# A hybrid encoder layer: nine groups' weight sums begun in the first six slots, and splits of weights moved behind the heads' chains

## The chip, the cores and the metric

The kernel runs on one core of a Trainium2 chip. The metric is the device time of one execution in microseconds (us). The engines are TensorE (PE, matmuls), VectorE (DVE), ScalarE (ACT), GpSimd (POOL) and SyncE (SP, which issues DMAs). They run their own instruction streams in order and wait for each other on semaphores.

## The reference

One layer on 512 prompt tokens and 32 new tokens, 1024 features, with the same weights:

```
h = rms_norm(x) @ w_in             # u, q, k, v (512 each), two gates (1024 each)
A = pooled means of u (windows 2, 4, 8, 16) minus u, a 128x128 map per group, @ w_pool_up
B = stick-breaking attention of 8 heads x 64: z = q k / 8, causal (s < t),
    a[t,s] = exp(log_sigmoid(z) + sum of log_sigmoid(-z) over the keys between s and t), a @ v, @ w_sb_up
x += (sigmoid(gate_a) * A + sigmoid(gate_b) * B) @ w_out
x += relu(rms_norm(x) @ w_up)^2 @ w_down          # 4096 hidden features
x += sigmoid(rms_norm(x) @ w_ple_gate) * (p @ w_ple_proj)
y = rms_norm(x)
```

The new tokens attend to 256 cached keys and to themselves. Keys, values and the pooling state are outputs too.

## The kernel before

Features lie on the partitions and the 544 tokens on the free axis. Every weight tile is 128 x 1024 numbers of fp32 (512 KB). Each is split into a high part in fp32r (an ACT copy, `w_hi`) and a low part (a DVE subtraction, `w_lo`). A product is then three matmul passes: high x high, high x low, low x high. In the code this pair of instructions is `split` (L845 on ACT, L1812 on DVE), with the tile's load in `raw` before it; there are two buffers of `raw` and four of `w_hi` and `w_lo`, so splits run three tiles ahead (`AHEAD`).

The first stage runs over four pairs of heads (`pair(i)`), each with eight weight tiles. Between its tiles TensorE computes, for each head hh of the pair:
- `scores` (L1381, L1382): z;
- `sums` (L1394 to L1406): the sums of the stick-breaking logs, as products with a triangle of -1;
- `outputs` (L1420, L1422): the product with the values.

The other engines run a chain between them. After the scores ACT computes a logarithm in three passes (`chain`, L921 to L925) and DVE makes the stick (`stick`, L1898). POOL masks its four diagonal blocks (`mask_diagonals`, L767). ACT and DVE make the high and low parts (`stick_hi` L930, `stick_lo` L1913 and L1915), and TensorE takes them up in `sums`. Then ACT takes the exponent (`prob`, L938), POOL masks it (L767 again), and ACT and DVE split it (`prob_hi` L943, `prob_lo` L1919) for `outputs`. Between these, ACT and DVE hold the splits of weights, in an order that is written out by hand in `pair`.

After the pairs come the pooling projection, the attention of the new tokens (POOL's mask L807, TensorE's sums L1559 to L1564), the projections and the mlp. Up and down projections (three of the four chunks) and the last gate use a 2x2 scheme with seven products in place of eight. For it, sums of quarters of the weights are needed. There are 16 groups (`SUM_GROUPS`), and in each four sums S1 to S4, which POOL has made by DMAs in device memory (`sums_t`): step 0 is four copies, steps 1 to 3 are two, one and one additions (DMAs that accumulate). Step k + 1 of a group needs step k landed. POOL issues them in slots. Slot k is issued in the loop over heads after the second mask of head k (k below 8), and later at paces set by TensorE. `sum_copies(k)` waits for all DMAs of the slots before k (`sums_made(k - 1)`), then the copies and the additions of slot k are issued. In the loop, the pooling means (`window_sums`, `window_mean`) stand around them:

```
for g in range(HEADS):
    pool.wait_ge(sp_done, g + 1)
    mask_diagonals(spm_done)
    ...
    pool.wait_ge(prob_done, g + 1)
    mask_diagonals(pm_done)
    sum_copies(g)
    sum_additions(g)
```

SP loads a finished sum like any weight tile, once the slot of its last step has landed (L679).

Of the kernel before, what the change touches and what calls it, by code (L numbers as in the profile page):

```python
# [19 lines left out]
HEADS = 8  # L20
# [12 lines left out]
S1_PER = 8  # L33
# [13 lines left out]
AHEAD = W_RING - 1  # L47
# [41 lines left out]

SUM_GROUPS = tuple((what, 2 * c + e) for c in range(CHUNKS) for what in ("up", "dn") if what == "up" or c < SEVENS  # L90
                   for e in range(2)) + (("ple", 0), ("ple", 1))

SUM_PAD = 16

# [203 lines left out]
def hybrid_step_kernel(nc, w_tiles, x_t, p_t, ck_t, cv, state_t, w_grp, vecs,  # L298
# [5 lines left out]
    with ctx:  # L304
# [217 lines left out]
        sums_in = sem("sums_in")  # L522
# [98 lines left out]

        def sum_slot(k):

            return [(i, k - i) for i in range(max(0, k - len(SUM_STEPS) + 1), min(k + 1, len(SUM_GROUPS)))]

        def sums_made(k):

            return 16 * sum(len(SUM_STEPS[step]) for j in range(k + 1) for _, step in sum_slot(j))
# [8 lines left out]
        def _(sp):  # L637
# [35 lines left out]
            def staged(n):  # L673
                name = STAGED_LOADS[n]
                wait_free(n)
                group, what = group_side(name) or (None, None)
                if what in SUMS:
                    nth = SUM_GROUPS.index(group)
                    sp.wait_ge(sums_in, sums_made(nth + len(SUM_STEPS) - 1))  # L679
                    sp.dma_start(raw_buf(n), sums_t[len(SUMS) * nth + SUMS.index(what), :, :])\  # L680
                        .then_inc(raw_in[raw_at(n)], 16)
                elif name[0] == "p":
                    sp.dma_start(raw_buf(n)[:, 0:TOK], p_t[:, name[1], :]).then_inc(raw_in[raw_at(n)], 16)
                else:
                    sp.dma_start(raw_buf(n), w_tiles[stored_tile(name), :, :]).then_inc(raw_in[raw_at(n)], 16)
# [21 lines left out]
        def _(pool):  # L707
# [104 lines left out]
            for c in range(CHUNKS):  # L812
                second = [NTH[("dn", c, s, 0)] for s in (0, 4)] if c < SEVENS else [NTH[("down", c, q)] for q in (0, 4)]
                paces += [(NTH[("up", 2 * c, 0)], NTH[("up", 2 * c + 1, 0)]), tuple(second)]
            for k, (copies, additions) in enumerate(paces, HEADS):
                if copies:
                    pool.wait_ge(full, copies)
                sum_copies(k)
                if copies:
                    pool.wait_ge(full, additions)  # L820
                sum_additions(k)
# [11 lines left out]
        def _(act):  # L833
# [126 lines left out]
            def pair(i):  # L960
# [18 lines left out]
                    split(AHEAD + 1)  # L979
                if not first:  # L980
                    prob(1, i - 1)
                split(AHEAD + 2, i, S1_PER, 2)
                if not first:
                    prob_hi(1, i - 1)
                chain(0, i)
                split(AHEAD + 3, i, S1_PER, 3)
                stick_hi(0, i)
                act.wait_ge(taken, 3 + i * S1_PER)
                act.dma_start(v_t[i, :, :], ev[:, 2, 0:TOK]).then_inc(kv_out[1], 16)
                act.wait_ge(vt_done, i + 1)  # L990
# [9 lines left out]
                    mean_hi(1)  # L1000
                split(AHEAD + 5, i, S1_PER, 5)
                prob(0, i)
                split(AHEAD + 6, i, S1_PER, 6)
                prob_hi(0, i)
                if last:
                    group_hi(0)
                    group_hi(1)
# [2 lines left out]
                    mean_hi(2)  # L1010
                    mean_hi(3)
                chain(1, i)
                split(AHEAD + 7, i, S1_PER, 7)
                if last:
                    group_hi(2)
                    group_hi(3)
                stick_hi(1, i)

            pair(0)
            with act.Fori(1, PAIRS - 1) as i:  # L1020
# [778 lines left out]
        def _(dve):  # L1799
# [189 lines left out]
            def pair(i):  # L1989
# [22 lines left out]
                else:  # L2012
# [5 lines left out]
                    dve.wait_ge(taken, 2 + i * S1_PER)  # L2018
                    dve.tensor_copy(kst[:, i, :], k[:, SEQ:TOK])
                    k_parts(i)  # L2020
                    split(AHEAD + 2, i, S1_PER)
                    prob_lo(1, i - 1)
                    dve.wait_ge(kv_out[1], 16 * i)
                    normed(2, v, i, S1_PER, pair_result(2, i)).then_inc(taken, 1)
                    dve.wait_ge(taken, 3 + i * S1_PER)
# [1 line left out]
                if not first:  # L2027
                    head_out(1, i - 1)
                    stick(0, i)
                    split(AHEAD + 3, i, S1_PER)  # L2030
                    stick_later(0, i)

                if not first:
                    pool_input(i)
                if first:
                    stick(0, i)
                    split(AHEAD + 3)
                    stick_later(0, i)
                stick_lo(0, i)
                dve.wait_ge(vhi_done, i + 1)  # L2040
                dve.tensor_tensor(v_parts[:, :, V_LO, :], o_heads, v_parts[:, :, V_HI, :], ALU.subtract)\
                   .then_inc(vlo_done, 1)
# [4 lines left out]

                    dve.wait_ge(mean_done, GROUPS)
                gate(1, i)
                split(AHEAD + 6, i, S1_PER)  # L2050
                if last:
                    mean_lo(0)
                    mean_lo(1)
                prob_lo(0, i)
                gate(2, i)
                if last:
                    group_lo(0)
                head_out(0, i)
                if last:
                    group_lo(1)  # L2060
                    mean_lo(2)
                    mean_lo(3)
                    gate(3, i)
                else:
                    split(AHEAD + 7, i, S1_PER)
                stick(1, i)
                if last:
                    group_lo(2)
                    group_lo(3)
                    stick_later(1, i)  # L2070
                    split(AHEAD + 7, i, S1_PER)
                    stick_lo(1, i)
                    for s in kv_out:
                        dve.wait_ge(s, 16 * PAIRS)
                else:
                    gate(3, i)
                    stick_later(1, i)
                    stick_lo(1, i)

            pair(0)  # L2080
            with dve.Fori(1, PAIRS - 1) as i:
# [472 lines left out]
```

## Time and profile before

| | us |
|---|---|
| median of 3 runs | 772.89 (772.16 to 772.94) |
| the profiled execution | 772.34 |
| its span | 770.6 |
| PE busy | 754.8 |
| DVE busy | 556.9 |
| ACT busy | 422.0 |
| POOL busy | 147.2 |

The span is the time from the first instruction to the last, and the profiled execution's own time lies 1.7 us above it. TensorE's granted clock over the span is 0.996 of full. POOL is seldom busy, but it issues 128 DMAs of 512 KB each for the sums; they have 35.5% of the 16 DMA engines' time over the span, and the queue of SP, mostly weight loads, has 35.6%.

### The profile page before, as it was taken

What the parts mean: (1) busy time and instruction counts of PE and PEld (TensorE: products, weight loads), DVE (VectorE), ACT (ScalarE), POOL (GpSimd) and SP (SyncE); (2) the same over time, 40 slices, a digit from 0 to 9 for tenths busy, and PEclk for the clock granted to TensorE, in tenths of its full rate; (3) what the DMA queues carried; (4) which work ended last, traced back from release to release, by engine and by line L of the source; (5) the groups of instructions that cost most, each with busy time, mean ns of one, the idle gap of its engine ahead of it and who ended that gap; (6) DMA issues with size and microseconds to landing.
All of it is one profiled execution on the core that took longest, in us unless ns stands there. A gap on an engine that the chain in (4) does not pass through costs nothing.

```text
span 770.6 us, 14459 instructions
## 1 busy us (share of the span) xinstructions
PE 754.8 (98%) x5902; PEld 746.2 (97%) x5902; DVE 556.9 (72%) x705; ACT 422.0 (55%) x524; POOL 147.2 (19%) x259
## 2 busy tenths in 40 slices
PE   9999999999999999999999999999999999999994
PEld 9999999999999999999999999999999999999993
DVE  6776556566567527588998669965998667677986
ACT  7545535435485442477674347634763356556575
POOL 1051342453471332021110111111101000000001
PEclk9999999999999999999999999999999999999998
DMA  7254848769779899988797989789776957342503
GB/s 242 93 181 140 233 147 224 225 193 262 218 179 265 259 242 275 292 267 262 213 299 270 236 329 251 282 232 354 207 243 201 278 185 217 105 117 66 204 1 116
DMA packets 49516, 165.78 MB, mean 215 GB/s; under 512 B 6320, under 2 KB 8368, under 8 KB 49456
## 3 DMA queue, kind: packets, MB, share of 16 engines
q1 hardware_dynamic: 28512, 94.16, 35.6%
q0 software_dynamic: 18688, 67.18, 35.5%
q10 hardware_dynamic: 2256, 3.60, 1.4%
q8 instruction: 43, 0.70, 0.4%
q14 instruction: 17, 0.14, 0.1%
HBM read 160.39 MB, written 71.63 MB: 301 GB/s over the span
## 4 chain that ended last, share of the span: by engine, by line
PE 90%; DVE 5%; ACT 3%; issue 1%; DMA 1%; SPq 0%; POOL 0%; POOLq 0%; DVEq 0%
PE psum L1646 23%; PE psum L1697 16%; PE psum L1345 14%; PE psum L1351 14%; PE psum L1348 14%; PE psum L1394 1%; PE psum L1422 1%; DMA xt<-x_t 1%; PE psum L1420 1%; PE psum L1382 1%; PE psum L1381 1%; ACT xt L1265 1%; PE psum L1401 1%; PE psum L1406 1%; ACT L879 0%
## 5 line engine op out<-in xcount | busy, mean ns | idle before, releaser
L853 ACT ACTIVATE w_hi<-raw_more 128x1024 fp32r<-128x1024 f32 x83 | 87.7, 1056 | 72.3 <-PE psum L1697 43.3
L1345 PE MATMUL psum<-a_hi,w_hi 128*128 128x272 f32 x576 | 120.6, 291 | 0.6 <-DVE w_lo L1812 0.5
L1820 DVE TENSOR_TENSOR w_lo<-raw_more,w_hi 128x1024 fp32r<-128x1024 f32 x83 | 101.1, 1222 | 26.1 <-ACT w_hi L853 25.7
L1351 PE MATMUL psum<-a_hi,w_lo 128*128 128x272 f32 x576 | 119.3, 289 | 0.0
L1348 PE MATMUL psum<-a_lo,w_hi 128*128 128x272 f32 x576 | 118.9, 288 | 0.0
L1646 PE MATMUL psum<-u_hi,w_hi 128*128 128x272 f32 x560 | 116.4, 289 | 1.0 <-ACT h_of L1097 1.0
L1646 PE MATMUL psum<-u_hi,w_lo 128*128 128x272 f32 x560 | 115.8, 289 | 0.0
L1646 PE MATMUL psum<-u_lo,w_hi 128*128 128x272 f32 x560 | 115.7, 288 | 0.0
L1345 PEld LDWEIGHTS psum<-a_hi,w_hi 128*128 128x128 f32 x576 | 90.3, 189 | 1.1 <-DVE w_lo L1812 0.7
L1348 PEld LDWEIGHTS psum<-a_lo,w_hi 128*128 128x128 f32 x576 | 90.5, 189 | 0.0
L1351 PEld LDWEIGHTS psum<-a_hi,w_lo 128*128 128x128 f32 x576 | 90.0, 189 | 0.0
L1646 PEld LDWEIGHTS psum<-u_hi,w_hi 128*128 128x128 f32 x560 | 87.9, 188 | 1.7 <-issue 1.2
L1646 PEld LDWEIGHTS psum<-u_lo,w_hi 128*128 128x128 f32 x560 | 88.3, 189 | 0.0
L1646 PEld LDWEIGHTS psum<-u_hi,w_lo 128*128 128x128 f32 x560 | 87.4, 188 | 0.0
L1812 DVE TENSOR_TENSOR w_lo<-raw,w_hi 128x1024 fp32r<-128x1024 f32 x41 | 51.2, 1250 | 43.3 <-ACT w_hi L845 43.1
L1820 DVE TENSOR_TENSOR w_lo<-raw,w_hi 128x1024 fp32r<-128x1024 f32 x44 | 53.6, 1222 | 19.2 <-ACT w_hi L853 12.3
L789 POOL DMA_DIRECT2D sums_t<-sums_t x32 | 27.5, 1013 | 207.1 <-PE psum L1646 87.9
L1348 PE MATMUL psum<-b_lo,w_hi 128*128 128x272 f32 x304 | 62.9, 288 | 0.0
L853 ACT ACTIVATE w_hi<-raw 128x1024 fp32r<-128x1024 f32 x39 | 41.2, 1056 | 36.0 <-PE psum L1697 21.6
L1345 PE MATMUL psum<-b_hi,w_hi 128*128 128x272 f32 x288 | 60.0, 290 | 0.0
L782 POOL DMA_DIRECT2D sums_t<-w_tiles x64 | 33.6, 535 | 135.5 <-DMA sums_t<-w_tiles 97.7
L1351 PE MATMUL psum<-b_hi,w_lo 128*128 128x272 f32 x288 | 59.4, 287 | 0.0
(287 smaller groups left out, 1553.0 us busy)
## 6 DMA issues: line engine op xcount, KB each, us to landing
sums_t<-w_tiles POOLq DMA_DIRECT2D x96, 512.0 KB, 8.2
raw<-w_tiles SPq DMA_DIRECT2D x63, 512.0 KB, 4.4
raw_more<-sums_t SPq DMA_DIRECT2D x42, 512.0 KB, 5.8
raw_more<-w_tiles SPq DMA_DIRECT2D x41, 512.0 KB, 4.5
sums_t<-sums_t POOLq DMA_DIRECT2D x32, 512.0 KB, 11.1
raw<-sums_t SPq DMA_DIRECT2D x22, 512.0 KB, 6.0
xt<-x_t SPq DMA_DIRECT2D x8, 272.0 KB, 5.7
y_t<-xt SPq DMA_DIRECT2D x16, 136.0 KB, 1.9
```

The lines of the kernel that those rows point to most:

```text
L782: pool.dma_start(sum_tile(i, what), sum_tile(i, of)).then_inc(sums_in, 16)
L789: pool.dma_start(sum_tile(i, what), sum_tile(i, of), accum_op=ALU.add).then_inc(sums_in, 16)
L853: act.activation(w_hi[:, t % W_RING, :, :].rearrange("p k c -> p (k c)"), src, ACT.Copy)\
L1265: act.activation(x, x, ACT.Copy, scale=g_fin[:, m:m + 1]).then_inc(xg_last, 1)
L1345: pe.matmul(base[:, h, :], w_hi[:, s, wk, :], at(hi, k, h * HALF, (h + 1) * HALF), start=(opens and q == 0), stop=False, skip_group_check= ...
L1348: pe.matmul(base[:, h, :], w_hi[:, s, wk, :], at(lo, k, h * HALF, (h + 1) * HALF), start=False, stop=False, skip_group_check=True)
L1351: mm = pe.matmul(base[:, h, :], w_lo[:, s, wk, :], at(hi, k, h * HALF, (h + 1) * HALF), start=False, stop=(closes and q == len(ks) - 1), s ...
L1381: pe.matmul(z, b_lo[:, keys], b_hi[:, both], start=(b != 3), stop=False, skip_group_check=True)
L1646: mm = pe.matmul(out[:, two, :], w_part[:, t % W_RING, 2 * k + two, :], u_part[:, op, k, :], start=(OPENS[s] and k == 0 and w_part is w_hi ...
L1697: mm = pe.matmul(out[:, two, :], w_part[:, t % W_RING, 2 * k + two, :], h_part[:, i * HALF:(i + 1) * HALF], start=(OPENS[s] and k == 0 and ...
L1812: dve.tensor_tensor(w_lo[:, s, :, :].rearrange("p k c -> p (k c)"), raw[:, t % RAW_RING, :], w_hi[:, s, :, :].rearrange("p k c -> p (k c)" ...
L1820: dve.tensor_tensor(w_lo[:, t % W_RING, :, :].rearrange("p k c -> p (k c)"), src, w_hi[:, t % W_RING, :, :].rearrange("p k c -> p (k c)"), ...
```

## The change

Group i began its four steps in slot i. A table now says in which slot each group begins: groups 0 to 8 begin in slots 0, 1, 2, 2, 3, 3, 4, 5, 5, and from group 11 on it is as before. The number of slots stays at 19. SP's wait for a sum follows the table.

```diff
+BEGINS = (0, 1, 2, 2, 3, 3, 4, 5, 5, 7, 9, 11, 12, 13, 14, 15)
+SLOTS = BEGINS[-1] + len(SUM_STEPS)
...
-            return [(i, k - i) for i in range(max(0, k - len(SUM_STEPS) + 1), min(k + 1, len(SUM_GROUPS)))]
+            return [(i, k - at) for i, at in enumerate(BEGINS) if 0 <= k - at < len(SUM_STEPS)]
...
-                    sp.wait_ge(sums_in, sums_made(nth + len(SUM_STEPS) - 1))
+                    sp.wait_ge(sums_in, sums_made(BEGINS[nth] + len(SUM_STEPS) - 1))
...
-            for k, (copies, additions) in enumerate(paces, HEADS):
+            for k, (copies, additions) in zip(range(HEADS, SLOTS), paces):
```

On ACT, in `pair`:

```diff
                 if not first:
                     prob(1, i - 1)
-                split(AHEAD + 2, i, S1_PER, 2)
+
                 if not first:
                     prob_hi(1, i - 1)
+                split(AHEAD + 2, i, S1_PER, 2)
                 chain(0, i)
+                stick_hi(0, i)
                 split(AHEAD + 3, i, S1_PER, 3)
-                stick_hi(0, i)
...
                 prob(0, i)
+                prob_hi(0, i)
                 split(AHEAD + 6, i, S1_PER, 6)
-                prob_hi(0, i)
...
                 chain(1, i)
-                split(AHEAD + 7, i, S1_PER, 7)
...
                 stick_hi(1, i)
+                split(AHEAD + 7, i, S1_PER, 7)
```

On DVE the same four splits go behind `prob_lo(1, i - 1)`, `stick_lo(0, i)`, `prob_lo(0, i)` and `stick_lo(1, i)`.

Two places in the order of instructions. First POOL, in the loop over heads, from the second mask of head 4 to the first mask of head 6 (`work`). The `sums_t` rows are slots 4 and 5, and the `gates` and `upad` rows are a pooling mean. Before:

```order
L767 AFFINE_SELECT work<-work 128x128 x4
L782 DMA sums_t<-w_tiles 128x1024 x4
L789 DMA sums_t<-sums_t 128x1024 x2
L789 DMA sums_t<-w_tiles 128x1024 x2
L757 TENSOR_SCALAR gates<-gates 128x551
L758 TENSOR_TENSOR gates<-gates,invc 128x8
L760 TENSOR_TENSOR upad<-gates,upad 128x559
L767 AFFINE_SELECT work<-work 128x128 x8
L782 DMA sums_t<-w_tiles 128x1024 x4
L789 DMA sums_t<-sums_t 128x1024 x2
L789 DMA sums_t<-w_tiles 128x1024 x2
L767 AFFINE_SELECT work<-work 128x128 x4
```

The same stretch of POOL now (the lines have moved down by four):

```order
L771 AFFINE_SELECT work<-work 128x128 x4
L786 DMA sums_t<-w_tiles 128x1024 x4
L793 DMA sums_t<-sums_t 128x1024 x3
L793 DMA sums_t<-w_tiles 128x1024 x4
L761 TENSOR_SCALAR gates<-gates 128x551
L762 TENSOR_TENSOR gates<-gates,invc 128x8
L764 TENSOR_TENSOR upad<-gates,upad 128x559
L771 AFFINE_SELECT work<-work 128x128 x8
L786 DMA sums_t<-w_tiles 128x1024 x8
L793 DMA sums_t<-sums_t 128x1024 x4
L793 DMA sums_t<-w_tiles 128x1024 x2
L771 AFFINE_SELECT work<-work 128x128 x4
```

Slot 4 has 11 DMAs where it had 8, and slot 5 has 14 where it had 8; the masks stand where they stood.

Second ACT, in the last pair, from the exponent of head 5 (L938) to the parts of head 6's stick. `w_hi` is a split of weights, the wide `b_hi` a high part, `work` the chain. Before:

```order
L938 ACTIVATE work<-psum 128x1280
L845 ACTIVATE w_hi<-raw 128x1024
L943 ACTIVATE b_hi<-work 128x1280
L921 ACTIVATE work<-psum 128x1280
L923 ACTIVATE work<-work 128x1280
L925 ACTIVATE work<-work 128x1280
L845 ACTIVATE w_hi<-raw 128x1024
L930 ACTIVATE b_hi<-work 128x1280
L932 ACTIVATE later_hi<-later 128x384
L989 DMA v_t<-ev 128x544
```

The same stretch of ACT now:

```order
L942 ACTIVATE work<-psum 128x1280
L947 ACTIVATE b_hi<-work 128x1280
L849 ACTIVATE w_hi<-raw 128x1024
L925 ACTIVATE work<-psum 128x1280
L927 ACTIVATE work<-work 128x1280
L929 ACTIVATE work<-work 128x1280
L934 ACTIVATE b_hi<-work 128x1280
L936 ACTIVATE later_hi<-later 128x384
L849 ACTIVATE w_hi<-raw 128x1024
L994 DMA v_t<-ev 128x544
```

Both splits have moved from ahead of an instruction that waits for POOL's mask to behind it.

## Rows read from the trace of the kernel before

**Rows 1.** The page's busy time of each engine.
```profile
PE 754.8 (98%) x5902; PEld 746.2 (97%) x5902; DVE 556.9 (72%) x705; ACT 422.0 (55%) x524; POOL 147.2 (19%) x259
```

**Rows 2.** Waits of PE: line <- releaser: us in total, times, longest.
```profile
PE psum L1345 <- issue: 1.1, 1, 1.1
...
PE psum L1345 <- DVE w_lo L1812: 0.5, 1, 0.5
```

**Rows 3.** DMA queues (packets, MB, share): 53:82, 82:111.5, then 140.4:169.9 us.
```profile
q0 software_dynamic: 576, 2.10, 20.9%
...
q0 software_dynamic: 928, 3.16, 40.2%
...
q0 software_dynamic: 1216, 4.21, 58.0%
q1 hardware_dynamic: 576, 2.10, 20.5%
q10 hardware_dynamic: 144, 0.28, 2.6%
```

**Rows 4.** Stretch 262 to 300 us: busy of each engine, PEclk, DMA share, GB/s.
```profile
262.00:300.00 38.00, 38.00 (x287) 35.52 (x286) 19.45 (x26) 16.93 (x25) 6.70 (x10) 1.00 0.97 236
```

**Rows 5.** Timeline of POOL, heads' stage: start, us, instruction [idle before <- releaser].
```profile
140.45 2.15 POOL L782 DMA_DIRECT2D sums_t<-w_tiles  x4
...
169.95 2.09 POOL L782 DMA_DIRECT2D sums_t<-w_tiles  x4
...
174.18 2.92 POOL L757 TENSOR_SCALAR gates<-gates 128x551 f32<-128x551 f32 x1
...
177.35 1.18 POOL L760 TENSOR_TENSOR upad<-gates,upad 128x559 f32<-128x559 f32 x1
...
210.60 1.95 POOL L767 TENSOR_SCALAR_AFFINE_SELECT work<-work 128x128 f32<-128x128 f32 x4 [6.14 <-DVE work L1898]
...
244.37 1.02 POOL L767 TENSOR_SCALAR_AFFINE_SELECT work<-work 128x128 f32<-128x128 f32 x4 [10.46 <-DVE work L1898]
...
256.03 2.09 POOL L782 DMA_DIRECT2D sums_t<-w_tiles  x4
...
267.74 0.44 POOL L807 TENSOR_SCALAR_AFFINE_SELECT work<-work 32x256 f32<-32x256 f32 x1 [6.18 <-DVE work L2111]
...
280.25 2.09 POOL L782 DMA_DIRECT2D sums_t<-w_tiles  x4 [4.04 <-DMA sums_t<-w_tiles]
```

**Rows 6.** Timeline of DVE, last pair of heads.
```profile
230.81 1.48 DVE L1919 TENSOR_TENSOR b_lo<-work,b_hi 128x1280 fp32r<-128x1280 f32 x1
...
246.20 1.22 DVE L1812 TENSOR_TENSOR w_lo<-raw,w_hi 128x1024 fp32r<-128x1024 f32 x1
...
248.74 0.55 DVE L1915 TENSOR_TENSOR later_lo<-later,later_hi 128x384 fp32r<-128x384 f32 x1
```

**Rows 7.** Timeline of ACT, last pair of heads.
```profile
212.58 1.27 ACT L930 ACTIVATE b_hi<-work 128x1280 fp32r<-128x1280 f32 x1 [2.62 <-POOL work L767]
...
226.03 1.24 ACT L938 ACTIVATE work<-psum 128x1280 f32<-128x1280 f32 x1
227.17 1.05 ACT L845 ACTIVATE w_hi<-raw 128x1024 fp32r<-128x1024 f32 x1
228.41 1.27 ACT L943 ACTIVATE b_hi<-work 128x1280 fp32r<-128x1280 f32 x1 [0.19 <-POOL work L767]
```

**Rows 8.** Timeline of PE: where it takes up heads 5, 6, 7 and new tokens.
```profile
194.05 0.40 PE L1394 MATMUL psum<-b_hi,negtri 128*128 128x512 f32 x1
...
232.67 0.39 PE L1420 MATMUL psum<-b_hi 128*128 128x512 f32 x1
...
251.19 0.40 PE L1394 MATMUL psum<-b_hi,negtri 128*128 128x512 f32 x1
...
268.34 0.59 PE L1559 MATMUL psum<-work,negtri 128*128 128x256 f32 x2
```

**Rows 9.** The last 6 us, columns as in rows 4.
```profile
765.00:771.00 6.00, 0.00 (x0) 0.00 (x0) 1.02 (x2) 0.00 (x0) 1.38 (x2) 0.50 0.53 186
```

More of the change, by code:

```diff
@@ L2020, in pair @@
                     k_parts(i)
+                    prob_lo(1, i - 1)
                     split(AHEAD + 2, i, S1_PER)
-                    prob_lo(1, i - 1)
                     dve.wait_ge(kv_out[1], 16 * i)
@@ L2029, in pair @@
                     stick(0, i)
-                    split(AHEAD + 3, i, S1_PER)
                     stick_later(0, i)
@@ L2036, in pair @@
                     stick(0, i)
-                    split(AHEAD + 3)
                     stick_later(0, i)
                 stick_lo(0, i)
+                split(AHEAD + 3, i, S1_PER)
                 dve.wait_ge(vhi_done, i + 1)
@@ L2049, in pair @@
                 gate(1, i)
-                split(AHEAD + 6, i, S1_PER)
                 if last:
@@ L2054, in pair @@
                 prob_lo(0, i)
+                split(AHEAD + 6, i, S1_PER)
                 gate(2, i)
@@ L2063, in pair @@
                     gate(3, i)
-                else:
-                    split(AHEAD + 7, i, S1_PER)
                 stick(1, i)
@@ L2070, in pair @@
                     stick_later(1, i)
+                    stick_lo(1, i)
                     split(AHEAD + 7, i, S1_PER)
-                    stick_lo(1, i)
                     for s in kv_out:
@@ L2078, in pair @@
                     stick_lo(1, i)
+                    split(AHEAD + 7, i, S1_PER)
             pair(0)
```

## The prediction

> **What bounds the kernel now.** I read the page's busy line first: TensorE is busy for 754.8 of 770.6 us [rows 1]. Then the list of what TensorE waits for. It is short, and the two entries on weight tiles of the stage that the change touches are 1.1 and 0.5 us [rows 2]. So TensorE is the bound, and there is next to nothing between its matmuls for a change to collect. An edit to the other engines can cost time, and hardly gain any.
>
> The change touches three engines that do not bound the kernel. The question is whether they still deliver in time. I therefore read the share of the DMA queues by stretches, the timeline of POOL during the heads, and the points at which TensorE consumes what POOL's masks release.
>
> **Part 1: the sums begun earlier.** A slot is a batch of DMAs that POOL issues after the second mask of a head. Before it issues a slot, POOL waits until every DMA of the earlier slots has landed. What stands behind this wait on POOL is the first mask of the next head, and ACT (`stick_hi`), DVE (`stick_lo`) and TensorE (`sums`) stand behind the mask. Counting the table's groups by step, slots 0 to 7 held 4, 6, 7, 8, 8, 8, 8, 8 DMAs and now hold 4, 6, 11, 14, 11, 14, 7, 7. Of these the copies are 8, 8, 4, 8, 0 in slots 2 to 6, and the additions 3, 6, 7, 6, 7.
>
> Price of one DMA in engine time (the share of the 16 engines times the stretch). Slot 0 is four copies: 20.9% of 29 us is 6.06 us, so 1.52 us each [rows 3]. Slot 1 adds two additions: 40.2% of 29.5 us is 11.86 us, so 2.9 us each. Slot 3 is four and four: 58.0% of 29.5 us is 17.1 us, so 2.76 us for an addition. I take 1.52 and 2.8.
>
> Room for them. When the queues are full the share is 0.97 [rows 4]. Weight loads and stores take 20.5% and 2.6% of a head's stretch [rows 3]. That leaves 0.97 - 0.23 = 0.74 for the sums. A check: eight DMAs, 4 x 1.52 + 4 x 2.8 = 17.3 us, should need 23.4 us. Slot 7 was issued at 256.03 and POOL's wait for it ended at 280.25, which is 24.2 us [rows 5]. The price holds.
>
> Slots 2 to 6 in the changed kernel, engine time over 0.74:
> - slot 2: 20.6 us, so 27.9 us. Slots come a head apart, 29.5 us (140.45 to 169.95) [rows 5], so from 111 to 139, just before slot 3's turn at 140.45.
> - slot 3: 29.0 us, so 39.2 us: to 179.7. Slot 4's turn is at 169.95, so POOL stands for 10 us.
> - slot 4: 25.7 us, so 34.8 us: to 214.5.
> - slot 5: 29.0 us, so 39.2 us: to 253.7.
> - slot 6: 19.6 us, so 26.5 us: to 280.2.
>
> Issuing costs POOL 0.53 us a DMA (from 169.95 to 174.18 for eight) [rows 5]: 5.8 us for slot 4, 7.4 us for slot 5, 3.7 us for slots 6 and 7.
>
> Now the masks, each against the moment when TensorE needs it:
> - Head 5. POOL is through with slot 4's issue at 185.5, the mean takes 4.4 us (174.18 to 178.53), the mask 1.0: 190.9. In head 7 DVE's last part ended 3.9 us after the mask's end (245.39 to 249.29), with a split of 1.22 us in between that is now moved out [rows 5, 6]. So 193.6 to 194.8, and TensorE wants it at 194.05 [rows 8]. Cost 0 to 0.7; I take 0.
> - Head 6. POOL waits to 214.5, issues to 221.9, where the mask began at 210.60: it is about 11 us late. ACT's work from that mask (212.58) to the exponent of head 6 (226.03) is back to back, 13.45 us [rows 7], and one split (1.05 us) now stands inside it. The exponent comes at 237.4 to 238.4, 11.9 us late. Slack behind it: ACT's copy ended at 229.68 and DVE took it up at 230.81, so 1.1 us, and TensorE began at 232.67 what was ready at 232.29, 0.4 us [rows 6 to 8]. TensorE stands for 11.9 - 1.5 = 10.4 us.
> - Head 7. Shifted by 10.4, the mask is due at 254.8. Slot 5 lands at 253.7 and slot 6 is issued until 257.4: 2.6 us late, against a slack of 1.9 us (249.29 to 251.19) plus 0.65 us from the moved split. Cost 0.
> - The new tokens. Their mask stands behind slot 7, which waits for slot 6: 280.2 + 3.7 + 0.4 = 284.3. TensorE needs it at 268.34 + 10.4 = 278.7, and had no slack before (mask ended at 268.18) [rows 5, 8]. That is 5.6 us. While TensorE stands, no new weights are asked for, 0.23 x 10.4 = 2.4 us of engine time, which brings the end of the queue forward by some 3 us. I take 2.6.
>
> Sum: 10.4 + 2.6 = 13.0 us. Each slot after the eighth waits for nothing of TensorE's, and TensorE never waited on a sum, so nothing is given back: the lighter queues from slot 8 on are worth 0.
>
> Bounds. If the sums get 0.79 of the engines (loads squeezed instead), slot 4 lands at 209.7, head 6 costs about 6 us and the new tokens 1: 7 us. If a DMA of the sums costs 10% more in the crowd, slot 4 lands at 221.7, head 6 costs 18 us and the sum comes to about 25 us.
>
> **Part 2: the splits moved behind the chains.** Each is 1.05 us on ACT and 1.22 us on DVE [rows 6, 7]. Moved, they bring `stick` and the parts behind it forward by 1 to 2 us. TensorE did not wait for any of them, so the gain is 0. The weights have three tiles of cover, 48 matmuls each at 287 in 38 us [rows 4], some 19 us. The price: on ACT a split now stands behind `stick_hi`, which waits for POOL's mask, so it no longer fills that wait. This is the 1.05 us in head 6 above. The only wait on a weight split, 0.5 us [rows 2], is for a tile whose split is not moved.
>
> **A rule about the clock.** In the last 6 us, with TensorE empty, the granted clock is 0.50, its lower level of 1.2 GHz [rows 9]. A stop of 10 us in the middle could do the same. No row shows how long the matmuls after such a stop would run slowly, so both ends are kept: 0, or one weight tile of 6 us at half speed, 6 us more. I take 0, because all rows with work on TensorE show 1.00 [rows 4]. The Trainium skill (TensorE: Matmul & The Clock Gate, "What's actually happening") says that an idle TensorE drops to the lower clock and returns only after sustained work; by that rule the first matmuls after the stop are slow too, and the sum would be nearer the upper end.
>
> **Rivals.**
> - A, no change. The slots drain in time. Slots 3 and 4 are 54.7 us of engine time and would have to land by about 204, so the sums would need 0.86 of the engines rather than 0.74. For it: a load can give way. Against: slot 7's 24.2 us. Then 772.9 us.
> - B, faster. The place is the two stops of TensorE on weight tiles, 1.1 and 0.5 us [rows 2]. If the earlier sticks and parts freed DVE in time for both, 772.9 - 1.6 = 771.3 us. It decides only if no mask is late at all. Against: the longer one is put down to no engine's work, and the split behind the shorter one isn't moved.
> - C, worse than the sum: the stops come with the half clock, or weight loads starve behind the fuller queue. 13.0 + 6, or 25 and more: 792 to over 801 us.
>
> **How the numbers follow.** The profiled execution took 772.34 us for a span of 770.6; the median of the runs is 772.89, 0.55 above. 772.89 + 13.0 = 785.9. Chances: forecast 0.70 (its own range 779 to 798), A 0.14, B 0.04, C 0.12. The range goes from 775, which takes in a sum of 2 us, to 801, the upper bound of 25 us with 3 more for the clock. Faster or slower means by over 0.2%, 1.5 us, about what a measurement of this kernel can tell from no change: faster 0.04, same 0.12, slower 0.84.
>
> **What would show it.** In the profile after: POOL waits for the sums' DMAs before slots 4, 5, 6 and 7 (10, 15, 15 and more us); the first mask of head 6 begins near 222; TensorE has a wait of some 10 us before the second head's outputs of the last pair, with ACT's exponent late, and a second one of 2 to 6 us at the sums of the new tokens; after that all as before, shifted. The forecast is wrong if POOL's waits are there but the masks still come in time, or if slot 3 takes much less than 39 us.

## The result and the profile after

| | before | after |
|---|---|---|
| median of the timed runs (six each, interleaved) | 773.88 us (772.16 to 776.51) | 799.68 us (798.21 to 802.04) |
| span of the profiled execution | 770.6 us | 797.8 us |
| PE busy | 754.8 us | 762.8 us |
| mean granted clock | 0.996 | 0.982 |

The changed kernel is slower: ratio 1.033, 95% interval 1.030 to 1.036, some 25.8 us. The forecast was 785.9 us, a loss of 13.0 us. The direction was right and the time lies in the range, but the loss is twice the forecast.

The page's busy line and queue line of the changed kernel, to be held against [rows 1]:

```profile
PE 762.8 (96%) x5902; PEld 752.4 (94%) x5902; DVE 558.9 (70%) x705; ACT 421.5 (53%) x524; POOL 144.3 (18%) x259
q0 software_dynamic: 18688, 67.18, 34.8%
```

TensorE runs the same 5902 matmuls and is busy 8.0 us longer with them. Its idle time grew from 15.8 to 35.0 us. So of the 27.2 us of span, 8.0 are the same matmuls at a slower clock and 19.2 are idle time; 1.7 of these lie behind the last matmul.

Where TensorE stops between 120 and 290 us. Columns: start, us, instruction, and in brackets the idle time just before it and its releaser.

```profile
147.45 0.79 PE L1425 MATMUL psum<-b_hi 128*128 128x512 f32 x1 [2.64 <-DVE b_lo L1924]
179.38 0.49 PE L1425 MATMUL psum<-b_hi 128*128 128x512 f32 x1 [0.64 <-DVE b_lo L1924]
214.85 0.80 PE L1425 MATMUL psum<-b_hi 128*128 128x512 f32 x1 [6.20 <-DVE b_lo L1924]
252.70 0.57 PE L1331 MATMUL psum<-mean_hi,b_hi 128*128 128x272 f32 x1 [6.17 <-DVE mean_lo L1985]
255.40 0.79 PE L1425 MATMUL psum<-b_hi 128*128 128x512 f32 x1 [1.00 <-DVE b_lo L1924]
270.05 0.49 PE L1350 MATMUL psum<-mean_hi,w_hi 128*128 128x272 f32 x2 [1.11 <-issue]
```

Only the last of these is in the kernel before [rows 2]. The others fall on two kinds of place: the outputs of a head (L1425; heads 3, 4 and 5, for 9.5 us together, then head 6), and the pooling projection (L1331), which takes `mean_lo`. With 0.64 us at head 0's outputs near 57 us, 1.00 at 255.40, and 0.37 us at the new tokens' cache, the new stops come to 17.7 us. Beyond 385 us all is as before and shifted by a constant 25.5 us (a matmul at 384.42 us is now at 409.94, one at 760.40 at 785.93). So the loss is made in the heads' stage and just after, and nothing is given back. The other 1.7 us of the 27.2 lie behind the last instruction that the trace shows: from its start to the end of the span it is 4.9 us before (765.66 to 770.6) and 6.6 now (791.19 to 797.8). What fills them is open.

POOL in the same stretch, to be held against [rows 5]:

```profile
180.10 2.10 POOL L786 DMA_DIRECT2D sums_t<-w_tiles  x4 [3.68 <-DMA sums_t<-w_tiles]
...
211.91 4.19 POOL L786 DMA_DIRECT2D sums_t<-w_tiles  x8
...
225.04 1.03 POOL L771 TENSOR_SCALAR_AFFINE_SELECT work<-work 128x128 f32<-128x128 f32 x4 [3.85 <-DVE work L1903]
...
228.50 0.57 POOL L747 DMA_DIRECT2D pool_t<-upad  x1
...
249.82 1.18 POOL L764 TENSOR_TENSOR upad<-gates,upad 128x559 f32<-128x559 f32 x1 [11.79 <-DMA pool_t<-upad]
250.95 1.56 POOL L771 TENSOR_SCALAR_AFFINE_SELECT work<-work 128x128 f32<-128x128 f32 x4
```

Two waits that the forecast counted on are not here: POOL issues slot 5 at 211.91 without a wait, and the first mask of head 6 (225.04) waits 3.85 us for DVE's stick, not for a slot. At 227.87 and 228.50 POOL issues the two stores of the pooling state (`pool_t`, 7.5 KB each), behind the 14 transfers of slot 5. The mean's last step (L764) overwrites what these stores read, and so waits for them to land. The second mask of head 6 stands behind it. DMAs in the chain that ended last, 125 to 300 us (start, us from issue to landing):

```profile
129.43 8.40 DMA raw<-w_tiles
...
151.28 28.53 DMA sums_t<-w_tiles
...
196.85 8.46 DMA raw<-w_tiles
...
228.50 21.18 DMA pool_t<-upad
...
279.36 7.36 DMA cvn<-cv
```

A store of 7.5 KB takes 21.18 us. In the kernel before, the median of these stores in the same stretch is 7.6 us. A load of weights takes 8.4 us near 130 us, where the median before was 5.5 (over 111 to 140 us). The 28.53 us are slot 3's last transfers, for which POOL waits before slot 4; the mean and the first mask of head 5 (191.21) stand behind.

ACT near 130 us. Two splits stand back to back, the next one waits for its load, and the exponent of the second head (L942) stands behind that and two short instructions:

```profile
126.44 1.99 ACT L849 ACTIVATE w_hi<-raw 128x1024 fp32r<-128x1024 f32 x2
131.17 1.29 ACT L972 ACTIVATE b_hi<-ev 64x512 fp32r<-64x512 f32 x2 [2.74 <-DVE ev L2002]
137.85 1.06 ACT L849 ACTIVATE w_hi<-raw 128x1024 fp32r<-128x1024 f32 x1 [5.39 <-DMA raw<-w_tiles]
...
142.15 1.24 ACT L942 ACTIVATE work<-psum 128x1280 f32<-128x1280 f32 x1
```

In the kernel before this exponent is at 138.17 us, 4 us earlier.

The clock around the longest stop. Columns as in [rows 4]: stretch, us, busy of PE, PEld, DVE, ACT, POOL with counts, granted clock, DMA share, GB/s.

```profile
248.00:252.00 4.00, 0.00 (x0) 0.00 (x0) 0.97 (x2) 0.00 (x0) 2.18 (x5) 0.73 0.06 21
252.00:260.00 8.00, 6.31 (x22) 5.73 (x23) 6.59 (x10) 3.31 (x4) 6.43 (x8) 0.50 0.78 140
260.00:264.00 4.00, 4.00 (x32) 3.91 (x32) 2.28 (x5) 3.12 (x7) 0.00 (x0) 0.99 1.05 270
```

After the stop TensorE works at the clock's lower level, 1.2 GHz, until about 260 us, and then back at 2.4. The stretch from the outputs to the pooling projection's weights took 12.42 us before (232.67 to 245.09) and takes 14.65 us now (255.40 to 270.05). Around the stop before 214.85 the mean clock was 0.83 over 210 to 230 us.

### The profile page after: what moved, and what is told of

It is laid out like the page before. It is cut to its first block, busy times and chain, and to the rows that moved or that the text cites. A ratio compares the mean times of both kernels' runs of the same rounds, so it can differ in the third digit from the quotient of the medians.

```text
span 797.8 us, 14459 instructions
## 1 busy us (share of the span) xinstructions
PE 762.8 (96%) x5902; PEld 752.4 (94%) x5902; DVE 558.9 (70%) x705; ACT 421.5 (53%) x524; POOL 144.3 (18%) x259
## 4 chain that ended last, share of the span: by engine, by line
PE 68%; DMA 10%; issue 7%; DVE 6%; ACT 5%; POOL 4%; POOLq 0%; ACTq 0%; DVEq 0%; SPq 0%
PE psum L1651 22%; PE psum L1702 16%; PE psum L1350 8%; PE psum L1356 8%; PE psum L1353 8%; DMA sums_t<-w_tiles 4%; DMA pool_t<-upad 3%; DMA raw<-w_tiles 3%; POOL work L771 1%; POOL sums_t L793 1%; DMA cvn<-cv 1%; POOL sums_t L786 1%; PE psum L1425 1%; DVE b_lo L1924 1%; ACT xt L1270 1%
## 5 line engine op out<-in xcount | busy, mean ns | idle before, releaser
L1817 DVE TENSOR_TENSOR w_lo<-raw,w_hi 128x1024 fp32r<-128x1024 f32 x41 | 53.6, 1316 | 33.6 <-ACT w_hi L849 33.6
L849 ACT ACTIVATE w_hi<-raw 128x1024 fp32r<-128x1024 f32 x46 | 47.8, 1050 | 41.2 <-DMA raw<-w_tiles 34.3
L1825 DVE TENSOR_TENSOR w_lo<-raw,w_hi 128x1024 fp32r<-128x1024 f32 x44 | 53.6, 1222 | 14.5 <-ACT w_hi L857 12.3
L857 ACT ACTIVATE w_hi<-raw 128x1024 fp32r<-128x1024 f32 x39 | 41.2, 1056 | 36.0 <-PE psum L1702 21.7
```

The lines of the kernel that those rows point to most:

```text
L849: act.activation(w_hi[:, s, :, :].rearrange("p k c -> p (k c)"), raw[:, t % RAW_RING, :], ACT.Copy).then_inc(whi_done, 1)
L857: act.activation(w_hi[:, t % W_RING, :, :].rearrange("p k c -> p (k c)"), src, ACT.Copy)\
L1817: dve.tensor_tensor(w_lo[:, s, :, :].rearrange("p k c -> p (k c)"), raw[:, t % RAW_RING, :], w_hi[:, s, :, :].rearrange("p k c -> p (k c)" ...
L1825: dve.tensor_tensor(w_lo[:, t % W_RING, :, :].rearrange("p k c -> p (k c)"), src, w_hi[:, t % W_RING, :, :].rearrange("p k c -> p (k c)"), ...
```

## The experiments

Each ratio is to the kernel before, timed in the same call on the same chip (its median there 774.66, 774.96, 774.66 and 774.73 us). Brackets hold the 95% interval. A ratio is not the quotient of the two medians, and differs from it by up to 0.2%. Times inside a run are of its one profiled execution.

### Which part costs: the sums alone, the splits alone

`e1_sums_only` is the kernel before with the table and what follows from it:

```diff
+BEGINS = (0, 1, 2, 2, 3, 3, 4, 5, 5, 7, 9, 11, 12, 13, 14, 15)
```

> Part 1 alone: the table of begins, all splits where they were before. Theory P (the prediction's): the sums cost everything, since masks come late behind fuller slots, so 1.03 to 1.033 of before, as with both parts. Theory Q (two causes that need each other: fuller queues make a weight load land after 8.4 us instead of 5.5, and the splits moved behind the chain issue two loads late and back to back at the turn of a pair): the stops of 2.6 and 6.2 us before the outputs of heads 3 and 5 (11.1 us in all in the changed kernel) shrink to under 2 us in sum, and the state transfer behind slot 5 still stops TensorE for some 7 us in the last pair: 1.012 to 1.018 of before.

`e2_splits_only` is the changed kernel with `BEGINS = tuple(range(16))`, which gives the slots of before.

> Part 2 alone: the splits where the changed kernel has them, group i beginning in slot i as before. Theory P: no change, 0.998 to 1.002 of before. Theory Q: the loads still go out late at the turn of a pair, but land after about 5.5 us, so the stops before the outputs of the second heads are 0.6 to 2 us each: 1.000 to 1.006. A third theory, that the moved splits alone are the cost, gives 1.015 or more.

Measured: the sums alone 799.49 us, 1.030 [1.027, 1.033]; the splits alone 775.05 us, 1.001 [0.999, 1.003]. The table alone is enough for nearly the whole loss, and the ratio is the one that theory P expected. But P's cause, masks late behind slots, is only a part of it, as the longest stop shows. TensorE's stops and POOL's rows in `e1_sums_only`:

```profile
207.88 0.56 PE L1423 MATMUL psum<-b_hi 128*128 128x512 f32 x1 [4.57 <-DVE b_lo L1922]
254.61 0.56 PE L1329 MATMUL psum<-mean_hi,b_hi 128*128 128x272 f32 x1 [14.72 <-DVE mean_lo L1983]
```

```profile
179.14 2.10 POOL L785 DMA_DIRECT2D sums_t<-w_tiles  x4 [9.44 <-DMA sums_t<-w_tiles]
...
213.27 4.19 POOL L785 DMA_DIRECT2D sums_t<-w_tiles  x8 [8.27 <-DMA sums_t<-w_tiles]
...
250.60 1.18 POOL L763 TENSOR_TENSOR upad<-gates,upad 128x559 f32<-128x559 f32 x1 [15.91 <-DMA pool_t<-upad]
```

Slots 3 and 4 land at 179.1 and 213.3 us, where the forecast had 179.7 and 214.5. The stop at the mean is 14.72 us, and its releaser is the state's store again (24.45 us from issue to landing).

The 4.57 us at the outputs of head 5 have another cause. ACT's stick part and exponent of head 5, first in the kernel before, then in `e1_sums_only`:

```profile
184.75 1.27 ACT L930 ACTIVATE b_hi<-work 128x1280 fp32r<-128x1280 f32 x1 [3.79 <-POOL work L767]
...
196.60 1.24 ACT L938 ACTIVATE work<-psum 128x1280 f32<-128x1280 f32 x1 [0.24 <-PE psum L1394]
```

```profile
191.31 1.28 ACT L933 ACTIVATE b_hi<-work 128x1280 fp32r<-128x1280 f32 x1 [10.67 <-POOL work L770]
...
202.66 1.24 ACT L941 ACTIVATE work<-psum 128x1280 f32<-128x1280 f32 x1
```

The mask, behind the wait for slot 3, and with it the stick part are 6.6 us late. At the sums TensorE waits only 0.74 us. But what ACT does between the stick part and the exponent takes 11.4 us, as before (11.9), so the exponent is 6.1 us late, and the outputs stand behind it. This is read from the rows; no run takes this delay away by itself.

### The state's stores out of the way

`e4_state_by_act`: the changed kernel, with the stores of the pooling state issued by ACT on its own queue.

```diff
-                pool.dma_start(pool_t[0, :, g, :], u[:, U_STATE - STATE:U_STATE]).then_inc(pool_out, 16)
-                pool.dma_start(pool_t[1, :, g, :], u[:, PADW - STATE:PADW]).then_inc(pool_out, 16)
...
+                act.dma_start(pool_t[0, :, i, :], upad[:, i, U_STATE - STATE:U_STATE]).then_inc(pool_out, 16)
+                act.dma_start(pool_t[1, :, i, :], upad[:, i, PADW - STATE:PADW]).then_inc(pool_out, 16)
```

> The changed kernel with the eight small transfers of the pooling state (7.5 KB each) issued by ACT, on its own queue, and not by POOL behind the sums. Theory Q: POOL's 11.8 us wait for the last of them goes, with it the stops of 6.2 and 1.0 us in the last pair and the lowered clock after them: 8 to 12 us less, 1.018 to 1.023 of before. Theory P (POOL stands because of the slots): unchanged, 1.033.

Measured: 790.18 us, 1.019 [1.016, 1.021], as expected. POOL's wait for the stores went from 11.79 to 5.05 us. The stop at L1331 is gone, and 1.20 us is left at the outputs behind it. The stop at head 5's outputs grew from 6.20 to 6.97 us.

`e5_sums_only_tails` is `e1_sums_only` with the state copied to a small buffer, from which it is stored, so that the mean waits for no store. `e6_both_tails` is the same edit in the changed kernel.

```diff
+                link(pool.tensor_copy(tails[:, g % 2, 0, :], u[:, U_STATE - STATE:U_STATE]))
+                pool.dma_start(pool_t[0, :, g, :], tails[:, g % 2, 0, :]).then_inc(pool_out, 16)
...
-                pool.wait_ge(pool_out, 32 * (g + 1))
```

> The table of begins alone (as in e1_sums_only), and POOL first copies the two pieces of pooling state into a small buffer, stores them from there, and no longer waits for that store before it makes the mean. Theory R (the state's store, 7.5 KB, lands behind the 14 transfers of slot 5 on POOL's own queue, 24.5 us after issue, and the mean and the mask of head 6 stand behind that wait): the 14.7 us stop goes down to what the late mask of head 6 alone leaves; e1's exponent for head 6 and the parts behind it put that at 5 to 10 us; 1.010 to 1.020 of before. Theory P (slots alone hold the masks): no gain, 1.030.

> The changed kernel with the same copy of the state and no wait for its store. Theory R: POOL's 11.8 us wait goes, so do the stops of 6.2 and 1.0 us in the last pair; 2.6 and 6.2 us before the outputs of heads 3 and 5 stay, and the new tokens' mask waits for slot 6 somewhat: 1.014 to 1.022 of before. Compared with e5_sums_only_tails it tells what the moved splits cost or bring once the state is out of the way. Theory P: 1.033.

Measured: 795.08 us, 1.028 [1.026, 1.030], a miss (1.010 to 1.020 was expected), and 791.21 us, 1.022 [1.020, 1.024], at the upper end of what was expected. TensorE's stops in `e5_sums_only_tails`:

```profile
208.35 0.80 PE L1427 MATMUL psum<-b_hi 128*128 128x512 f32 x1 [4.57 <-DVE b_lo L1926]
241.71 0.37 PE L1333 MATMUL psum<-mean_hi,b_hi 128*128 128x272 f32 x1 [0.95 <-DVE mean_lo L1987]
243.73 0.50 PE L1427 MATMUL psum<-b_hi 128*128 128x512 f32 x1 [1.02 <-DVE b_lo L1926]
256.27 0.49 PE L1352 MATMUL psum<-mean_hi,w_hi 128*128 128x272 f32 x2 [1.11 <-issue]
278.30 3.68 PE L1543 MATMUL psum<-qbd,ckt 128*128 128x64 f32 x16 [5.67 <-DMA cvn<-cv]
```

This kernel has the masks that are late behind slots, and not the store. Its outputs of head 6 begin at 243.73, 11.1 us later than the 232.67 of [rows 8], where 10.4 was forecast. But TensorE does not lose these 11.1 us in one stop at head 6. It stood 4.57 us at head 5, and at head 6's sums it was already 8.7 us late (232.18, where the kernel before has 223.47); 0.95 and 1.02 us came at the mean and the outputs. A new stop of 5.67 us appears at the load of the cached values (issued at 265.60 by ACT, 12.66 us to landing in the full queues). The stop at the mean fell from 14.72 to 0.95 us, and the median by only 4.4 us (the ratios, 1.030 and 1.028, by less).

`e6_both_tails` is the changed kernel without the store. TensorE stops for 1.02 us at head 0's outputs, 2.21 at head 3's, 8.21 at head 5's and 1.06 at the cached values. At head 6's outputs it doesn't stop:

```profile
215.81 0.79 PE L1429 MATMUL psum<-b_hi 128*128 128x512 f32 x1 [8.21 <-DVE b_lo L1928]
...
247.60 0.39 PE L1429 MATMUL psum<-b_hi 128*128 128x512 f32 x1
```

POOL's wait before slot 6 ends 38.1 us after slot 5's issue (212.88 to 250.96).

`e8_seven_eight_later`: the changed kernel with groups 7 and 8 begun in slot 7, which leaves 6 and 3 DMAs in slots 5 and 6, ahead of the state's stores, and puts 13 into slot 7, behind them (the expectation counts 9).

```diff
-BEGINS = (0, 1, 2, 2, 3, 3, 4, 5, 5, 7, 9, 11, 12, 13, 14, 15)
+BEGINS = (0, 1, 2, 2, 3, 3, 4, 7, 7, 7, 9, 11, 12, 13, 14, 15)
```

> The changed kernel with groups 7 and 8 begun in slot 7 and not in slot 5, so that slot 5 holds 6 transfers and not 14, slot 6 holds 3 and slot 7 holds 9; slots 2 to 4 stay at 11, 14, 11. Theory R (what counts is what stands in POOL's queue ahead of the last state store): the store lands some 8 us after issue, the 6.2 and 1.0 us stops go, those before the outputs of heads 3 and 5 stay: 1.012 to 1.020 of before. Theory S (what counts is the sum of transfers in the heads' stage, which is nearly the same up to slot 7): 1.028 or more.

Measured: 790.08 us, 1.020 [1.019, 1.022], at the upper end of what was expected. The stops at the mean and at head 6's outputs are gone; those of 2.53, 0.80 and 5.20 us at the outputs of heads 3, 4 and 5 stay.

`e9_six_more_in_slot5` goes the other way: the kernel before, with six extra copies of 512 KB behind slot 5 and nothing else.

```diff
+                if g == 5:
+                    for n in range(6):
+                        pool.dma_start(spare_t[n, :, :], w_tiles[T_MLP + 40 + n, :, :]).then_inc(spare_in, 16)
```

> The kernel before, and POOL issues six more plain copies of 512 KB (weight tiles into unused device memory) behind slot 5; no slot waits for them. Nothing else is changed, so they act only through the queue. Theory R: slot 5 is then 26.4 us of engine time, 35.7 us at a share of 0.74, so from 198.9 to about 234.6; the last state store, issued at 214.3, lands behind it some 20 us later instead of 7.6, the mean and the mask of head 6 end near 237 instead of 228.4, and TensorE stops for about 7 us before the products of the last pair: with the clock 1.009 to 1.014 of before. Theory S (only the waits for whole slots count): no slot is waited for longer than before by more than a few us, 1.000 to 1.003.

Measured: 782.77 us, 1.011 [1.008, 1.014], as expected; the stop is 5.3 us where about 7 was. The median load of weights over 200 to 240 us is 8.1 us, as in the kernel before. The stop, then the store's way in the chain of waits:

```profile
237.42 0.57 PE L1333 MATMUL psum<-mean_hi,b_hi 128*128 128x272 f32 x1 [5.34 <-DVE mean_lo L1987]
```

```profile
214.97 18.23 DMA pool_t<-upad
```

So the mechanism works in the kernel before, with no other change around it: six transfers on one queue ahead of a 7.5 KB store cost 8 us of the kernel's time.

### The last split of a pair

`e3_split7_back`: the changed kernel with the last split of a pair back where it was, ahead of the second head's stick parts, on ACT and on DVE. `e11_tails_split7_back` is the same edit on top of `e6_both_tails`.

```diff
+                split(AHEAD + 7, i, S1_PER, 7)
                 stick_hi(1, i)
-                split(AHEAD + 7, i, S1_PER, 7)
```

> The changed kernel with one split, the last of each pair (AHEAD + 7), put back to its place before the second head's stick on ACT and DVE. Theory Q: this parts the two splits at the turn of the pair, the loads go out some 10 us apart again, and the stops before the outputs of heads 1, 3 and 5 go from 0.6, 2.6 and 6.2 us to under 1 us each; with the clock that they cost, 8 to 14 us less: 1.015 to 1.023 of before. Theory P: that split bears on no mask, so 1.033 as it is.

> As e6_both_tails (both parts of the change, state copied aside), with the last split of a pair back ahead of the second head's stick. Theory Q (two splits back to back at the turn of a pair send two loads late): the stops of 2.2 and 8.2 us before the outputs of heads 3 and 5 shrink to 0 to 1 and 3 to 4, as in e3_split7_back, and now nothing behind takes the gain back: 1.013 to 1.018 of before, against 1.022. If something later takes it back (the exponent of head 6 or the new tokens' loads): 1.020 to 1.024.

Measured: 797.59 us, 1.028 [1.025, 1.031], and 790.46 us, 1.021 [1.018, 1.024]. The stop near 147 us went and the one before the last pair fell, in `e3_split7_back` to 3.35 us. But the next stop grew: 11.47 us at the mean in place of 6.17, and in `e11_tails_split7_back` 0.96 at the mean, 1.70 at the outputs and 1.77 at the cached values. The first ratio lies between the two theories, the second is the one expected if something later takes the gain back. What takes it back in `e3_split7_back` is the queue. POOL's turn for slot 5 comes earlier, but it waits 7.09 us for slot 4 and issues slot 5 at 211.78, against 211.91. The store, issued 4.0 us earlier (224.49 against 228.50) behind the same slot, lets POOL go on only 1.3 us earlier (248.48 against 249.82).

### A milder table, with and without the moved splits

These kernels begin the groups less densely. Slots 2 to 7 hold 11, 10, 9, 9, 8, 8 DMAs:

```diff
+BEGINS = (0, 1, 2, 2, 3, 4, 5, 6, 7, 8, 9, 11, 12, 13, 14, 15)
```

`e10_one_early` has it with all the moved splits.

> The changed kernel with a milder table, begins 0, 1, 2, 2, 3, 4, 5, 6, 7, 8, 9, 11 and on: one group early, slots 2 to 7 hold 11, 10, 9, 9, 8, 8 transfers. By the prices (1.52 and 2.8 us, share 0.74) slot 3 lands at 171.4, 1.4 us after slot 4's turn, slot 4 at 198.6 and slot 5 at 226.1. Theory R (a backlog costs only when it reaches past a turn): no stop over 1.5 us, 0.999 to 1.004 of before. If any extra transfer costs in proportion (19 of them up to the end of slot 5 cost 3.3%, here 8): 1.012 or more.

Measured: 782.19 us, 1.010 [1.008, 1.012], a miss. TensorE stopped for 2.60 us before 148.02 and 2.00 before 211.15. The next two kernels ask whether the table or the splits did it: `e13_one_early_old_splits` has the splits of before, and `e14_one_early_split7_back` all moved but the last of a pair.

> The kernel before with the milder table (groups begin in slots 0, 1, 2, 2, 3, 4, 5, 6, 7, 8, 9, 11 ...; slots 2 to 7 hold 11, 10, 9, 9, 8, 8 DMAs) and with the splits of weights where the kernel before has them. It is the fourth cell beside that table with all splits moved (ratio 1.010). Theory P: the fuller queue and the moved splits act together: with the splits behind the chains, two loads of weights are asked for back to back and late, and what a slightly fuller queue adds to their landing reaches TensorE; with the splits in their old places it does not. Ratio 0.998 to 1.004, and TensorE's stops of 2.6 us (near 147) and 2.0 us (near 210) are gone. Theory Q: the table alone does it, as it did with the full table; the splits have no part. Ratio 1.007 to 1.012, with stops of 2 us and more at the second heads' outputs.

> The changed kernel with the milder table and with only the last split of a pair back in its old place, ahead of the second head's stick parts; the other three splits stay behind the chains. P, with the turn of a pair as the place (the last two splits of a pair back to back): the stop of 2.6 us near 147 goes, and the ratio comes to 1.001 to 1.006. P, with the split behind the exponent's high part as the place: no change from 1.010. Q: 1.007 to 1.012 too, with the stop near 147 still there.

Measured: 773.78 us, 0.9985 [0.997, 1.000], and 773.83 us, 0.999 [0.998, 1.000]. Within 0.2% both are the kernel before, and the stops of 2.60 and 2.00 us are gone. So it needed both, the table and this one split; whether this split would do it without the other three was not tried. ACT at the turn of a pair, first in `e10_one_early`:

```profile
127.05 1.99 ACT L849 ACTIVATE w_hi<-raw 128x1024 fp32r<-128x1024 f32 x2
131.79 1.29 ACT L972 ACTIVATE b_hi<-ev 64x512 fp32r<-64x512 f32 x2 [2.74 <-DVE ev L2002]
138.43 1.06 ACT L849 ACTIVATE w_hi<-raw 128x1024 fp32r<-128x1024 f32 x1 [5.36 <-DMA raw<-w_tiles]
...
142.72 1.24 ACT L942 ACTIVATE work<-psum 128x1280 f32<-128x1280 f32 x1
```

And in `e14_one_early_split7_back`:

```profile
122.12 1.04 ACT L849 ACTIVATE w_hi<-raw 128x1024 fp32r<-128x1024 f32 x1
...
128.55 1.04 ACT L849 ACTIVATE w_hi<-raw 128x1024 fp32r<-128x1024 f32 x1
132.03 1.29 ACT L972 ACTIVATE b_hi<-ev 64x512 fp32r<-64x512 f32 x2 [2.44 <-DVE ev L2002]
133.80 1.06 ACT L849 ACTIVATE w_hi<-raw 128x1024 fp32r<-128x1024 f32 x1 [0.48 <-DMA raw<-w_tiles]
...
138.81 1.24 ACT L942 ACTIVATE work<-psum 128x1280 f32<-128x1280 f32 x1 [0.31 <-PE psum L1399]
```

A split frees a buffer of `raw`, and there are two. With the last split of the pair at 122.12, the load that follows it is asked for 5 us earlier, and ACT waits 0.48 us for it. Behind the stick parts, it stands at 127.05 with the next one right behind it, the load that follows it is issued at 130.04 and lands 8.37 us later, and the exponent of the second head stands behind its split. In `e2_splits_only` the queue was emptier (4.0 us a load, median over 111 to 140 us; 5.5 in the kernel before), and there the same order costs nothing.

### The clock

`e7_sums_only_fill` and `e12_fill_64` are `e1_sums_only` with 56 and 64 idle products ahead of the pooling projection (`group(0)`), which keep TensorE busy in part of the stop. Nothing reads their results.

```diff
+                    pe.wait_ge(vlo_done, PAIRS)
+                    for _ in range(56):
+                        pe.matmul(o_ps[:, 0:P], negone[:, :].bitcast(F32), negone[:, :].bitcast(F32), start=True,
+                                  stop=True, skip_group_check=True)
```

> The table of begins alone (as in e1_sums_only), and TensorE does 56 idle products of 128 x 128 into an unused bank just before the pooling group product at which it stands for 14.7 us. They should take about 12.4 us at full clock (8 halves of 136 columns took 0.94 us), so they fit into the stop. Theory C (the stop also costs the clock, which is granted at 0.81 and 0.68 in the 20 us stretches at 230 and 250): the granted clock stays near 1.00 there and 3 to 5 us come back, 1.024 to 1.027 of before. If the clock's fall costs nothing, or the products themselves hold TensorE up: 1.030 or more.

> As e7_sums_only_fill, with 64 idle products in place of 56, so that they end at most 0.3 us before the 14.7 us stop does. In e7 the stops of 2.0 and 1.1 us left behind them still let the clock fall to 0.50 between 256 and 262. Theory C (the clock costs about 2.8 us per long stop: 15.3 us from the outputs to the pooling projections in e1 against 12.4 in the kernel before): with no gap left the clock stays at 1.00 and that stretch takes 12.4 us again, 1.025 to 1.027 of before. If the products are simply added: 1.030 or more.

Measured: 797.26 us, 1.029 [1.027, 1.031], and 797.64 us, 1.030 [1.028, 1.033], against 1.030 [1.027, 1.033] for `e1_sums_only`. Both miss what theory C expected. With 56 the stops left were 2.04 and 1.12 us, and the clock was still 0.50 from 256 to 260 us. With 64 it stayed at 1.00. The same 4 us, first in `e1_sums_only`, then in `e12_fill_64`:

```profile
256.00:260.00 4.00, 3.60 (x14) 3.12 (x13) 2.62 (x4) 0.71 (x1) 3.74 (x5) 0.50 1.06 235
```

```profile
256.00:260.00 4.00, 3.48 (x23) 3.30 (x24) 3.56 (x6) 1.13 (x2) 2.47 (x3) 1.00 1.00 255
```

The stretch from the outputs to the pooling projection's weights took 15.30 us in `e1_sums_only` and 12.54 us in `e12_fill_64`, as in the kernel before (12.42). The profile shows 2.8 us recovered behind this one stop, and its span is 2.9 us shorter (799.1 to 796.2). The medians differ by 1.9 us in the same direction (799.49 and 797.64), the ratios by nothing. The intervals are 4 to 5 us wide, so whether the filling pays is not shown.

## Where the prediction held, and where it failed

- **The queue's price: right.** 1.52 us a copy, 2.8 us an addition, 0.74 of the engines for the sums. Slots 3 and 4 were to land at 179.7 and 214.5 us and landed at 179.1 and 213.3 with the sums alone. Slot 5 was to need 39.2 us and needed 38.1 in `e6_both_tails`. In the changed kernel slot 3 landed at 180.1. POOL's waits were shorter than forecast (3.7 us before slot 4, none before slots 5 to 7), as its turns came late themselves.
- **Head 5, "I take 0": wrong, and the first step that failed.** The mask, at 190.2 us with the sums alone (190 forecast), and the wait at the sums, 0.74 (0 to 0.7), were right. But the prediction followed the mask only to the sums. It did not follow it on through ACT's work to the exponent and the outputs, as it did for head 6. On that path TensorE stopped for 4.57 us with the sums alone. In the changed kernel ACT waits another 5.58 us there for a load, behind the two splits that now stand back to back; the exponent comes at 209.63 us and the stop is 6.20 us. The 2.64 us at head 3's outputs are of the same kind. The 0.64 us at heads 0 and 4 were not taken apart.
- **Head 6, "TensorE stands for 11.9 - 1.5 = 10.4 us": right for the path, wrong for the changed kernel.** With the sums alone and the store out of the way the exponent came at 237.44 (237.4 to 238.4 forecast) and the outputs 11.1 us late, most of it lost before, at head 5 and in the slower clock behind it. In the changed kernel this path did not bind: TensorE and the stick were late themselves, POOL did not wait before slot 5, and without the store there is no stop at head 6's outputs (`e6_both_tails`).
- **The store, at no cost in the working: the second step that failed.** The forecast took what POOL issues between its two masks as unchanged. The two small stores of the state stand on the same queue as slot 5 and land 21 to 24 us after they are issued, in place of 7.6. Behind them stand the mean, the pooling projection and the second mask. It made stops of 6.2 us in the changed kernel and 14.7 us with the sums alone. That the changed kernel loses 7.2 us near the place where 10.4 was forecast is luck: another wait made them.
- **Head 7, cost 0: right.** No stop falls there. **The new tokens, 2.6 us: wrong as to mechanism.** Their mask (293.26) waited for DVE's work and not for a slot, and TensorE waited 0.37 us, for the load of cached values.
- **The moved splits, "so the gain is 0", at a price of 1.05 us: right for the time of this change, wrong as a statement on the edit.** Alone they gave 1.001. With the milder table, one of the four costs 1.1% (1.010 against 0.999). The cover of "three tiles" was right for TensorE's weights and beside the point: the split delays ACT's exponent, not the weights. With the full table the times can't tell whether the two parts add up (1.030 and 1.001 alone, 1.033 together); the stops moved from the mean (14.72 to 6.17 us) to the outputs of heads 3 and 5 (4.57 to 8.84).
- **The clock, "I take 0": wrong.** TensorE was busy for 8.0 us more with the same instructions, just above the upper end of 6 us that was kept. That end was for one stop, and there were three (2.6, 6.2, and 6.2 with 1.0 behind it). The one at the pooling projection cost 2.2 us in the stretch behind it alone (12.42 to 14.65). The Trainium skill (TensorE: Matmul & The Clock Gate, "What's actually happening") says that the matmuls after an idle time run at the lower clock; the windows above agree (0.50 from 252 to 260 us).
- **Rivals.** A and B fell with the first measurement. C named the half clock and weight loads slowed by the fuller queue, and by its time (792 to over 801 us) it is the case that came. It did not name the store, and TensorE waited for no weight there: the slow loads held up ACT's exponent.

The sum by measured terms: outputs of heads 0, 3, 4 and 5 10.1 us, mean 6.2, outputs of head 6 1.0, cached values 0.4, clock 8.0, together 25.7, where the last matmul is 25.5 us later. The other 1.7 us of the span lie behind the last instruction, and the prediction has no term for them.

Of the kernels tried, none is faster than the kernel before by more than 0.2%.

## What to carry to other kernels

When more transfers go into a queue, list everything that is issued on it later, small stores first: here a store of 7.5 KB took 21 us in place of 7.6, and whatever waited for it (an in-place update and a mask) inherited the backlog. Follow a late result to every matmul that needs it, not only to the first. An instruction order that was free while a load landed in 4 to 6 us cost 1% when it landed in 8, so an order measured alone should be measured again together with the change that fills the queue; and count 2 to 3 us more for the clock with each stop of TensorE of some us (an estimate, from 2.2 and 2.8 us at the mean and 8.0 us for all stops).

## What the runs showed of the hardware

- A store of 7.5 KB took 7.6 us behind a slot of eight transfers of 512 KB, 18.2 us with six plain copies more, and 21.2 and 24.5 us behind a slot of 14. Issued on ACT's queue, with the same 14 on POOL's, these stores took 13.0 us, against 20.4 on POOL's (medians over 200 to 240 us): another queue helped, and still left more than the 7.6. The Trainium skill (DMA: Bandwidth & Descriptors, "Queues, rings and completion order") says that each DMA engine alternates between queues packet by packet, and, of the queues of SP and ACT, that it takes the descriptors of one ring in order. If the second holds for POOL's queue too, it fits the 21 us; that a store on another ring should still need 13 us does not follow from the first, and is open.
- A weight load of 512 KB, on a queue of its own, took 5.5 us where the software queue had 48.8% of the engines' time, and 8.5 us where it had 72.5% (medians over 111 to 140 us, the kernel before and the changed one).
- The clock after short stops: in `e10_one_early`, behind one stop of 2.60 us, it was 0.57 from 148 to 152 us. In `e7_sums_only_fill`, behind stops of 2.04 and 1.12 us, 2 us apart, it was 0.50 from 256 to 260 us. In `e5_sums_only_tails`, with stops of 0.95 and 1.02 us, it was 1.00 from 235 to 255 us.
